# Recurrence: the second tile's units write across partition halves

## The reference, cut to what matters

```python
def step(state, inp):                      # state: 64x64 of each head
    r_t, w_t, k_t, v_t, kk_t, b_t = inp
    sa = einsum("bhvk,bhk->bhv", state, -kk_t)
    state = (state * w_t[:, :, None, :] + sa[..., None] * b_t[:, :, None, :]
             + v_t[..., None] * k_t[:, :, None, :])
    y_t = einsum("bhvk,bhk->bhv", state, r_t)
    return state, y_t
```

## Time and profile before

| | us |
|---|---|
| median of 3 runs | 2822.99 |
| lowest, highest | 2822.29, 2823.99 |
| profiled execution | 2821.47 |
| its span | 2819.7 |
| the recurrence within it | 385.1 to some 531 |

### The profile page before, as it was taken

The page is one execution under the profiler, slowest core; times in us unless marked ns, Lnnn a source line. Parts: engine busy times, 40 slices in busy tenths (PEclk is TensorE's granted clock), DMA queues, the critical chain, the costliest instruction groups (busy, mean ns, idle before and its releaser), DMA issues. The chain is left out here.

```text
span 2819.7 us, 40275 instructions
## 1 busy us (share of the span) xinstructions
PE 2496.6 (89%) x16378; PEld 1614.5 (57%) x16378; DVE 1116.6 (40%) x2453; ACT 549.8 (19%) x1340; POOL 323.5 (11%) x330
## 2 busy tenths in 40 slices
PE   9999999898999998987887789999999988877882
PEld 5444579646888655555554455666664555455551
DVE  3572667766555653211111154444545531111114
ACT  1311455210000011111111131322331111111112
POOL 3321000310000211111111000000003011111110
PEclk9999999999999999999999989999999999999996
DMA  3111010230113136999999970000103499999997
GB/s 115 38 38 53 1 47 4 70 119 31 45 45 116 69 134 261 406 419 420 420 420 420 384 285 16 17 24 8 65 31 135 179 382 419 420 420 420 420 421 296
DMA packets 111034, 566.11 MB, mean 201 GB/s; under 512 B 22000, under 2 KB 22160, under 8 KB 59376
## 3 DMA queue, kind: packets, MB, share of 16 engines
q1 hardware_dynamic: 85808, 506.87, 44.6%
q0 software_dynamic: 20144, 38.79, 3.6%
q10 hardware_dynamic: 4896, 17.83, 1.6%
HBM read 529.06 MB, written 65.01 MB: 211 GB/s over the span
## 5 line engine op out<-in xcount | busy, mean ns | idle before, releaser
L3009 PE MATMUL ex__h_ps<-all__arena,ex__xT 128*64 128x256 f32 x3392 | 529.7, 420 | 167.0 <-DMA all__arena<-in_w_gate 108.5
L3009 PEld LDWEIGHTS ex__h_ps<-all__arena,ex__xT 128*64 128x64 f32 x3392 | 338.9, 152 | 337.8 <-issue 224.9
L3052 DVE COPY ex__ysb<-ex__y_ps 128x512 f32<-128x512 f32 x64 | 44.3, 692 | 630.3 <-PE ex__y_ps L3029 629.8
L3009 PE MATMUL ex__h_ps<-mo__wx,ex__xT 128*64 128x256 f32 x704 | 175.0, 406 | 0.0
L3029 PE MATMUL ex__y_ps<-b__w,ex__hT 128*64 128x512 f32 x672 | 152.1, 592 | 0.9 <-ACT ex__hT L3046 0.9
L3173 POOL DMA_INDIRECT b__rows<-s_hn,mo__queue x60 | 60.6, 1010 | 760.9 <-PE ex__x_ps L3002 746.0
L2351 PE MATMUL cm__acc<-all__arena,cw__w 128*128 128x260 f32 x576 | 136.0, 386 | 2.6 <-PEq L84 2.3
L2351 PE MATMUL cm__acc<-all__arena,cm__sums 128*128 128x260 f32 x576 | 134.3, 383 | 0.0
L2351 PEld LDWEIGHTS cm__acc<-all__arena,cw__w 128*128 128x128 f32 x576 | 110.4, 192 | 20.4 <-issue 3.3
L2351 PEld LDWEIGHTS cm__acc<-all__arena,cm__sums 128*128 128x128 f32 x576 | 109.5, 190 | 17.2 <-issue 0.3
L2731 PE MATMUL hd__o<-all__arena 128*128 128x128 f32 x704 | 96.5, 282 | 14.1 <-ACT all__arena L2794 13.6
(11 more groups left out here) (538 smaller groups left out, 4392.5 us busy)
## 6 DMA issues: line engine op xcount, KB each, us to landing
all__arena<-in_w_gate SPq DMA_DIRECT2D x106, 1024.0 KB, 27.8
all__arena<-in_w_up SPq DMA_DIRECT2D x106, 1024.0 KB, 27.6
b__w<-in_w_down SPq DMA_DIRECT2D x84, 1024.0 KB, 27.8
all__arena<-in_w_down SPq DMA_DIRECT2D x22, 1024.0 KB
mo__wx<-in_w_gate SPq DMA_DIRECT2D x22, 1024.0 KB, 28.0
mo__wx<-in_w_up SPq DMA_DIRECT2D x22, 1024.0 KB
mo__wx<-in_w_down SPq DMA_DIRECT2D x22, 1024.0 KB
all__arena<-s_ys SPq DMA_DIRECT2D x16, 1024.0 KB, 8.5
```

The costliest lines, as they stand in the source:

```text
L3009: last = nc.tensor.matmul(h_ps[half, c, DE * b:DE * b + DE], xT[:, b, k, half], slots[n][:, c, k], start=(k == 0), stop=(k == KT - 1))
L3052: return nc.vector.tensor_copy(ysb[:, b, 512:], y_ps[:, 1])
```

## The change

Units 1 and 3 (tile 1, `crosses(u)` is 1) no longer keep to their half. `both` gets two more arguments: `held` says that the operands of head h now lie in the other half, `flip` that the output goes to the half opposite the operands. In the crossing these units flip, so that their products stand on the two quarters that units 0 and 2 leave free; the first squares and MV are done within the half in which the operands now lie; the levels n = 0 to 3 flip each time, the last level and TAV don't, and the gr products flip back, so that the state step is as before. Where products of two units may stand on four quarters, their calls alternate in the order: `PAIRS` are units (0, 1) and (2, 3).

Where a level flips, `inv` can't be added in place, since the product comes out in the other half. PE therefore also multiplies `inv` by the identity and accumulates pw inv onto it in PSUM (one call more), and ACT copies the sum to `inv` (semaphore `inv_copied`) in place of DVE's addition. A pair's calls stand behind the waits of both of its units.

```diff
--- before.py
+++ after.py
@@ -982,6 +982,7 @@
                  "v_own", "crossed", "masked", "tok_out", "inv_init", "sq_done", "pw_out", "mv_done", "mv_out", "inv_done",
                  "inv_out", "tav_done", "tav_out", "gr_done", "gr_out", "hz_out", "zx_done", "z_out", "z_done", "y_out",
                  "var_ready", "rooted", "y_in", "y_turned", "weighed"))
+        inv_copied = ph.sem("inv_copied")
 
         def tile_of(u):
             return u % 2
@@ -997,6 +998,17 @@
 
         def blocks(bank, first, count=1):
             return bank[:, HALF * first:HALF * (first + count)]
+
+        PAIRS = ((0, 1), (2, 3))
+
+        def crosses(u):
+            return u % 2
+
+        def inverse_ready(i, u, n):
+
+            if n == SQ - 1:
+                return inv_out, i * 3 * U + 2 * U + u + 1
+            return (inv_copied if crosses(u) else inv_out), i * (2 * U if crosses(u) else 3 * U) + 2 * n + u // 2 + 1
 
         with nc.Block() as block:
 
@@ -1055,7 +1067,7 @@
                         dve.wait_ge(mv_done, i * U + u + 1)
                         V.tensor_copy(big[:, u, MV], blocks(Y[u], 0)).then_inc(mv_out, 1)
                     for n in range(SQ):
-                        for u in range(U):
+                        for u in range(U) if n == SQ - 1 else (0, 2):
                             dve.wait_ge(inv_done, i * U * SQ + U * n + u + 1)
                             V.tensor_tensor(inv[:, u], inv[:, u], blocks(Y[u], 0), ALU.add).then_inc(inv_out, 1)
                     if i:
@@ -1092,11 +1104,16 @@
                         act.wait_ge(masked, i * U + u + 1)
                         nc.scalar.copy(big[:, u, A_:B_ + 1].rearrange("p a b -> p (a b)"), blocks(Y[u], 1, 4)).then_inc(tok_out, 1)
                     for n in range(SQ):
-                        for u in range(U):
-                            act.wait_ge(sq_done, i * U * SQ + U * n + u + 1)
-                            kept = 2 if n < SQ - 1 else 1
-                            nc.scalar.copy(pw[:, u, 0:kept].rearrange("p a b -> p (a b)"), blocks(X[u], 0, kept)
-                                           ).then_inc(pw_out, 1)
+                        kept = 2 if n < SQ - 1 else 1
+                        for pair in PAIRS:
+                            if n:
+                                u = pair[1]
+                                act.wait_ge(inv_done, i * U * SQ + U * (n - 1) + u + 1)
+                                nc.scalar.copy(inv[:, u], blocks(Y[u], 0)).then_inc(inv_copied, 1)
+                            for u in pair:
+                                act.wait_ge(sq_done, i * U * SQ + U * n + u + 1)
+                                nc.scalar.copy(pw[:, u, 0:kept].rearrange("p a b -> p (a b)"), blocks(X[u], 0, kept)
+                                               ).then_inc(pw_out, 1)
                     for u in range(U):
                         act.wait_ge(tav_done, i * U + u + 1)
                         nc.scalar.copy(tav[:, u].rearrange("p a b -> p (a b)"), blocks(X[u], 0, 2)).then_inc(tav_out, 1)
@@ -1114,11 +1131,11 @@
             @block.tensor
             def _(pe):
 
-                def both(out, weights, moving, start=True, stop=True):
+                def both(out, weights, moving, held=0, flip=0, start=True, stop=True):
 
                     for h in range(2):
-                        hp = slice(HALF * h, HALF * h + HALF)
-                        last = nc.tensor.matmul(out[hp], weights[hp], moving[hp], start=start, stop=stop)
+                        rows, cols = (slice(HALF * x, HALF * x + HALF) for x in (h ^ held, h ^ held ^ flip))
+                        last = nc.tensor.matmul(out[cols], weights[rows], moving[rows], start=start, stop=stop)
                     return last
 
                 def turn_output(i, u):
@@ -1126,54 +1143,75 @@
                     return both(blocks(X[u], 4), yn[:, u], idh[:])
 
                 for i in range(ROUNDS):
-                    for u in range(U):
-                        if i:
-
-                            pe.wait_ge(z_out, (i - 1) * U + u + 1)
-                            pe.wait_ge(y_out, (i - 1) * U + u + 1)
-                        if i > 1:
-                            pe.wait_ge(weighed, (i - 2) * U + u + 1)
-                        r, a, b, k, val = (feature(i, u, n) for n in (R, A, B, K, V_IN))
-                        for n, (rows, cols) in enumerate(((b, r), (b, a), (k, r), (k, a))):
-                            both(blocks(X[u], n), rows, cols)
-                        both(blocks(Y[u], 0), a, b)
-                        for n, src in enumerate((a, val, k, b)):
-                            last = both(blocks(Y[u], 1 + n), src, idh[:])
-                        last.then_inc(crossed, 1)
+                    for pair in PAIRS:
+                        for u in pair:
+                            if i:
+
+                                pe.wait_ge(z_out, (i - 1) * U + u + 1)
+                                pe.wait_ge(y_out, (i - 1) * U + u + 1)
+                            if i > 1:
+                                pe.wait_ge(weighed, (i - 2) * U + u + 1)
+                        for n, (rows, cols) in enumerate(((B, R), (B, A), (K, R), (K, A))):
+                            for u in pair:
+                                both(blocks(X[u], n), feature(i, u, rows), feature(i, u, cols), 0, crosses(u))
+                        for u in pair:
+                            both(blocks(Y[u], 0), feature(i, u, A), feature(i, u, B), 0, crosses(u))
+                        for n, src in enumerate((A, V_IN, K, B)):
+                            for u in pair:
+                                last = both(blocks(Y[u], 1 + n), feature(i, u, src), idh[:], 0, crosses(u))
+                                if src == B:
+                                    last.then_inc(crossed, 1)
                     for u in range(U):
                         pe.wait_ge(masked, i * U + u + 1)
-                        both(blocks(X[u], 0), big[:, u, LT], pw[:, u, 0])
-                        both(blocks(X[u], 1), pw[:, u, 0], big[:, u, LT]).then_inc(sq_done, 1)
+                        both(blocks(X[u], 0), big[:, u, LT], pw[:, u, 0], crosses(u))
+                        both(blocks(X[u], 1), pw[:, u, 0], big[:, u, LT], crosses(u)).then_inc(sq_done, 1)
                     for u in range(U):
                         pe.wait_ge(tok_out, i * U + u + 1)
-                        both(blocks(Y[u], 0), big[:, u, MT], big[:, u, V_]).then_inc(mv_done, 1)
+                        both(blocks(Y[u], 0), big[:, u, MT], big[:, u, V_], crosses(u)).then_inc(mv_done, 1)
                     for n in range(SQ):
-
-                        for u in range(U):
-                            pe.wait_ge(pw_out, i * U * SQ + U * n + u + 1)
-                            if n:
-                                pe.wait_ge(inv_out, i * U * SQ + U * (n - 1) + u + 1)
-                            else:
-                                pe.wait_ge(inv_init, i * U + u + 1)
-                                pe.wait_ge(mv_out, i * U + u + 1)
-                            both(blocks(Y[u], 0), pw[:, u, 0], inv[:, u]).then_inc(inv_done, 1)
-                            if n < SQ - 1:
-                                last = both(blocks(X[u], 0), pw[:, u, 1], pw[:, u, 0])
-                                if n < SQ - 2:
-                                    last = both(blocks(X[u], 1), pw[:, u, 0], pw[:, u, 1])
-                                last.then_inc(sq_done, 1)
+                        half_turn = n < SQ - 1
+                        for pair in PAIRS:
+                            for u in pair:
+                                pe.wait_ge(pw_out, i * U * SQ + U * n + u + 1)
+                                if n:
+                                    own, count = inverse_ready(i, u, n - 1)
+                                    pe.wait_ge(own, count)
+                                else:
+                                    pe.wait_ge(inv_init, i * U + u + 1)
+                                    pe.wait_ge(mv_out, i * U + u + 1)
+                            held = [crosses(u) * (1 - n % 2) for u in pair]
+                            flip = [crosses(u) * half_turn for u in pair]
+                            for u, at, f in zip(pair, held, flip):
+                                if f:
+                                    both(blocks(Y[u], 0), idh[:], inv[:, u], at, f, True, False)
+                                    both(blocks(Y[u], 0), pw[:, u, 0], inv[:, u], at, f, False, True).then_inc(inv_done, 1)
+                                else:
+                                    both(blocks(Y[u], 0), pw[:, u, 0], inv[:, u], at, f).then_inc(inv_done, 1)
+                            for x in range(0 if n == SQ - 1 else 1 if n == SQ - 2 else 2):
+                                for u, at, f in zip(pair, held, flip):
+                                    last = both(blocks(X[u], x), pw[:, u, 1 - x], pw[:, u, x], at, f)
```

(30 more changed lines are left out.)

## The result

The changed kernel takes 2827.2 us (median of 20 runs, 2823.8 to 2830.3), the kernel before beside it 2822.3 (20 runs, 2820.0 to 2826.0): a ratio of 1.0016, interval 1.0010 to 1.0022. It is slower by 4.9 us (interval 2.8 to 6.2), just inside the 5.6 us that the prediction counted as no change; the forecast was 15.5 us faster. The loss lies in the recurrence: by the timelines it took 145.5 us (385.2 to 530.7) and takes 150.5 (385.0 to 535.5). The two profiled executions as wholes are 3.3 us apart (spans 2819.7 and 2823.0).

The account below looks back on a forecast made before the run. PE was taken as the bound. Gains of 0.56 (crossing), 0.64 (levels) and 1.00 (gr with state step) over eight rounds, plus 1.0 in round 0, made 18.6; less 3.1, 15.5 us: 2807.5 us, forecast 2800 to 2814, 8-in-10 range 2799 to 2820.

Parts of the forecast that it names:

- about 3 are stalls of PE that I can't place ... 1 us: Recurrence: about 3 us of unplaced PE stalls cost more if queues empty sooner; 1 us taken off the gain.
- Issue is no limit: PE instruction issue: eight weight loads at L3558 start within 0.05 us; the change wants 16 records in 0.117 us.
- 1.16 a level: Levels n=0 to 3: round trip becomes the bound, 1.16 us a level, 1.03 for n=3; gain 0.64 a round.
- The clock was to fall in a quarter of the rounds: After the crossing: thin PE work lowers the clock, 1.2 us each time; 2.1 us taken off with round trips.
- rival B: Clock falls in every round, 8x1.5 = 12 us off the 18.6 gain: 2816 us; chance 0.10.
- rival A: Every paired call: off-diagonal quarters don't run beside diagonal ones, a crossing pair takes 0.233 us: 2833 us; chance 0.11.
- 1.37 and 0.12 forecast: gr products: two pairs take 1.37 us in place of 2.74 and start 0.12 later; gain 1.24 a round.
- the state step: State step: four DVE operations stand ahead of z, which starts 0.76 us after PE's end; loss 0.24 a round.
- The crossing's 0.56: Crossing to MV: pairing frees 2.1 us of PE, but readers don't follow; gain 0.56 us a round.
- C: Round trips longer than forecast, levels and crossing give nothing, only gr gains: 8 us, 2815; chance 0.07.
- D: Half concurrency, a pair of calls at 0.155 us: 12 us gain, 2812, inside the forecast's own range.

Follow-up runs that it names:

- e5: Changed kernel with only those PE waits that the others don't imply, 240 PE instructions less in all: 2822.3 us, ratio 0.9999 to the kernel before.
- e6: Changed kernel's crossing and gr pairs with the levels of the kernel before, implied PE waits left out: 2817.6 us, ratio 0.9980 to the kernel before.
- e3: Changed kernel without the 64 identity products, 512 PE instructions less: 2827.1 us, ratio 1.0017 to the kernel before.
- e7: Paired crossing and gr, levels on two quarters, few waits, plus calls merged in levels n=0 to 2: 2815.9 us, ratio 0.9977 to the kernel before.

## Why the prediction was wrong

**Which step failed.** The term "about 3 are stalls of PE that I can't place ... 1 us". Those stalls were the page stops: three pieces of "issue", 1.2 us, the tip of a floor that lay 0.3 us a page below the work. Halving the work of a page of crossing or gr to 1.9 us ran into it, and "issue" went from 1.2 to 18.6 us. So the supply of PE's instructions, which the prediction had ruled out as a limit and put at nothing, is the step that failed. I had asked "Issue is no limit" of eight weight loads at L3558; that shows a rate over 8 instructions and nothing of a rate over 256.

**The levels.** The second term that failed. 1.16 a level was forecast and 1.35 measured, where the kernel before has 1.40. With all five levels, and without the stops, a round lost some 0.3 us where 0.64 less was forecast. Of the 0.19 a level, 0.12 is the string of four waits, as e5 shows; about the rest is ACT, which takes the second powers 0.82 after the pair's start (447.65 to 448.47) and not 0.72.

**A slip in the sum.** The clock was to fall in a quarter of the rounds, two of eight, at 1.2 us and the round trips behind it. That is 2.4 or more, and rival B reckons with 1.5 a round, 3; the sum took off 2.1. That moves the forecast by less than 1 us.

**What held.** Four quarters run at once: the crossing calls of two units together start every 0.117 us, so rival A is false. The rule of the Trainium skill ("TensorE: Matmul & The Clock Gate", Part 3, The mechanism), by which a weight load overlaps with matmuls in flight only when the row group differs, does not hold for these tiles: the two units of a pair share both row groups.

```profile
459.62 0.34 PE L1138 MATMUL rwc__x<-all__arena,V__bb 64*64 64x64 f32 x8
459.76 0.33 PE L1138 MATMUL rwc__x<-V__kkb,V__bb 64*64 64x64 f32 x8
459.87 0.33 PE L1138 MATMUL rwc__x<-all__arena 64*64 64x64 f32 x8
```

gr took 1.50 (1.37 and 0.12 forecast) and the state step 1.73 (1.72). The crossing's 0.56 is real where the stops leave it: the shortest round of e6 took 3.50 and 1.93 for crossing and squares with MV, 5.43 in place of 6.00, and 15.52 as a whole, where the forecast's terms without the levels give 16.93-1.56 = 15.37. Its one stop, 1.14 us, lies between crossing and squares, where the forecast has PE idle for the masks, and the page before it and its first were among the shortest, 3.12 and 3.27; the next best round of e6 took 1.0 more:

```profile
474.10:477.60 3.50, 2.36 (x148) 2.22 (x145) 3.25 (x18) 1.08 (x5) 0.35 (x2) 1.00 0.02 5
477.60:479.53 1.93, 1.83 (x52) 1.56 (x51) 1.24 (x7) 1.65 (x7) 0.93 (x3) 1.00 0.03 8
474.10:489.62 15.52, 14.22 (x531) 13.45 (x529) 12.26 (x63) 9.08 (x37) 1.28 (x4) 1.00 0.02 4
```

**The other rivals.** B: the clock did not fall in every round. Beside the fall at the stage's head there is one more in the rounds, 394.7 to 398.1, at the end of the longest stop (2.56 us, up to 395.26). That the stop causes it is likely and not shown. C named the right place, the levels, and nearly the right size, nothing gained; that the crossing would lose to the supply it did not have. D's pair at 0.155 isn't seen.

**The account.** From a forecast of 15.5 us less to 5 us more in the stage are 20.5 us. 16.4 of "issue" beyond the 1 us allowed, and 0.19 x 3 x 8 = 4.6 of the levels n=0 to 2, make 21. The match is partly luck. The two overlap with each other and with waits that would have stood anyway. And the levels cost more than the 4.6: all five of them, without the stops, took 0.3 us a round more than before where 0.64 less was forecast, which is 7.5 in all.

**Open.** Why e3 gains nothing as a median though its profile is shorter, why e7 gives back most of the "issue" it saves (the clock is a candidate for both), what share of the "issue" time is lost and what share would have been waited for anyway, and whether the change would pay under a full supply: no run had one.

## What to carry to other kernels

Look at the rate of instructions before you make an engine's work shorter: in an unrolled stream, 256 PE instructions (a 64x64 `f32` call of two halves is eight) took 3.45 us each in a row, and what stands well above that for its array time can be halved only down to there. Slack of one page is handed on only up to some 0.7 us. And of several waits in a row leave out those that others imply, and put the one that comes last at the end: it was worth 0.12 us a level here.

## What the hardware showed that I had not expected

- Pages of 256 PE instructions: one every 3.45 us where PE waits for nothing else, with the fetch of a page starting 1.1 us after the page before it began and the page beginning 2.35 us after that; in the changed stage 2.2 to 2.8. Single pages went down to 2.79 behind slower ones.
- A fetch packet of 16 KB itself takes 0.9 to 1.5 us there; no record shows what the rest of the 2.2 to 2.8 is.
- Two 64x64 calls on all four quarters together take what one takes on two, 0.117 us, and the next pair follows at once.
- The granted clock is at the 1.2 GHz level at the head of the stage. In the burst of 4-column calls it stayed there for 37.5 us, with PE busy for 3.59 of 3.73 us; in the four-quarter burst of 64-column calls it was at 2.4 GHz in each window from 402.30 on, with a stop of 1.36 us in every 3.45.
